# VectorE's order in the SSD steps of a two-layer diffusion backbone: the expert slots of a step ahead of its three results

## What is computed

```python
xdt = x * dt[..., None]
a = dt * a_neg;  a_cum = cumsum(a)
lmat = exp(segsum(a))                        # the decay tile of a chunk, 128 x 128 for each head
scores = einsum('bclhn,bcshn->bhcls', ch, bh) * lmat
y_diag = einsum('bhcls,bcshp->bclhp', scores, xdt)
states = einsum('bclhn,bhcl,bclhp->bchpn', bh, decay_states, xdt)
y_off  = einsum('bclhn,bchpn,bhcl->bclhp', ch, states_before, exp(a_cum))
# PEER, for each block of 128 tokens
act = gelu(einsum('thkd,td->thk', u_tab[idx], hb))
out = einsum('thk,thkd->td', gate * act, v_tab[idx])
```

## Time and profile before

| | us |
|---|---|
| median of 3 runs | 4722.75 (4718.49 to 4725.61) |
| the profiled execution | 4715.53 |
| its span on the core | 4713.7 |
| TensorE busy | 3706.6 (79%), mean granted clock 0.934 |
| VectorE busy | 3311.5 (70%) |
| ScalarE busy | 763.8 (16%) |
| GpSimd busy | 1482.1 (31%) |
| SSD steps of the sample group, layer 1 | 590.5 to 702.0 |
| SSD steps of the prompt group, layer 2 | 2407.9 to 2437.2 |
| SSD steps of the sample group, layer 2 | 2892.3 to 3003.8 |

### The profile page before, as it was taken

The page is one execution under the profiler, slowest core; times in us unless marked ns, Lnnn a source line. Parts: engine busy times, 40 slices in busy tenths (PEclk is TensorE's granted clock), DMA queues, the critical chain, the costliest instruction groups (busy, mean ns, idle before and its releaser), DMA issues.

```text
span 4713.7 us, 35962 instructions
## 1 busy us (share of the span) xinstructions
PE 3706.6 (79%) x10742; PEld 1837.6 (39%) x10742; DVE 3311.5 (70%) x8263; ACT 763.8 (16%) x2285; POOL 1482.1 (31%) x1284
## 2 busy tenths in 40 slices
PE   6578677988787778788878696788977878777776
PEld 6464434643232222235535453355422323222222
DVE  1636885677888868754574767767788787786665
ACT  0121125221010010010121112351210100101001
POOL 0001131223544435422222011213244544444432
PEclk9789798999999999999989897899999999999999
DMA  8244465777999999999979354658699999999998
GB/s 275 84 131 161 164 233 201 274 269 311 419 420 410 422 415 420 419 371 391 367 255 352 125 196 163 224 205 305 248 398 421 408 421 421 413 421 418 400 421 338
DMA packets 342147, 1497.69 MB, mean 318 GB/s; under 512 B 31424, under 2 KB 176448, under 8 KB 178112
## 3 DMA queue, kind: packets, MB, share of 16 engines
q0 software_dynamic: 184320, 1342.26, 71.0%
q1 hardware_dynamic: 157632, 153.13, 10.1%
HBM read 1491.97 MB, written 3.31 MB: 317 GB/s over the span
## 4 chain that ended last, share of the span: by engine, by line
DMA 32%; PE 31%; DVE 28%; issue 5%; ACT 4%; SPq 1%; POOL 0%; DVEq 0%; ACTq 0%; POOLq 0%
DMA uv_ring<-uv,expert_index 20%; PE expert_acc L752 13%; DMA arena<-uv,expert_index 10%; DVE uv_ring L1340 6%; PE rotating L989 3%; PE rotating L781 3%; DVE diag L1349 3%; PE rotating L815 2%; DVE arena L1340 2%; PE rotating L961 2%; DVE arena L1722 2%; DVE arena L1509 2%; DVE arena L1715 2%; DMA w_ring<-w_ada 1%; PE rotating L731 1%
## 5 line engine op out<-in xcount | busy, mean ns | idle before, releaser
L752 PE MATMUL expert_acc<-uv_ring,diag 128*128 128x512 f32 x3452 | 1736.2, 634 | 391.7 <-DVE diag L1349 382.5
L705 POOL DMA_INDIRECT uv_ring<-uv,expert_index x943 | 1091.2, 1157 | 2678.9 <-PE expert_acc L752 1942.5
L752 PEld LDWEIGHTS expert_acc<-uv_ring,diag 128*128 128x128 f32 x3452 | 632.0, 198 | 1354.1 <-DVE diag L1349 811.1
L1340 DVE CUSTOM_DVE_ANT_0 uv_ring<-uv_ring,arena 128x1024 f32<-128x1024 f32 x687 | 839.7, 1223 | 259.8 <-DMA uv_ring<-uv,expert_index 256.6
L752 PE MATMUL expert_acc<-arena,diag 128*128 128x512 f32 x1348 | 677.5, 627 | 220.2 <-DVE diag L1349 189.9
L1049 ACT ACTIVATE gelu<-u_dot 128x1 f32<-128x1 f32 x1280 | 258.8, 203 | 2789.1 <-DVE u_dot L1340 2788.5
L1349 DVE TENSOR_SCALAR diag<-const_mats,expert_gate,gelu 128x128 f32<-128x128 f32 x1200 | 436.4, 364 | 272.1 <-ACT gelu L1049 184.1
L705 POOL DMA_INDIRECT arena<-uv,expert_index x337 | 390.7, 1159 | 509.0 <-PE expert_acc L752 491.0
L752 PEld LDWEIGHTS expert_acc<-arena,diag 128*128 128x128 f32 x1348 | 238.0, 194 | 643.8 <-DVE diag L1349 422.0
L1340 DVE CUSTOM_DVE_ANT_0 arena<-arena 128x1024 f32<-128x1024 f32 x337 | 412.5, 1224 | 95.8 <-DMA arena<-uv,expert_index 94.8
L1340 DVE CUSTOM_DVE_ANT_0 uv_ring<-uv_ring,prompt_rows 128x1024 f32<-128x1024 f32 x256 | 312.4, 1220 | 104.7 <-DMA uv_ring<-uv,expert_index 104.2
(11 more groups left out here) (211 smaller groups left out, 2895.7 us busy)
## 6 DMA issues: line engine op xcount, KB each, us to landing
w_ring<-w_ada SPq DMA_DIRECT2D x66, 512.0 KB
w_ring<-w_in SPq DMA_DIRECT2D x64, 512.0 KB
w_ring<-w_pq SPq DMA_DIRECT2D x64, 512.0 KB
w_ring<-w_out SPq DMA_DIRECT2D x32, 512.0 KB
uv_ring<-w_ada SPq DMA_DIRECT2D x30, 512.0 KB, 5.8
uv_ring<-uv,expert_index POOLq DMA_INDIRECT x943
arena<-b_ada SPq DMA_DIRECT2D x48, 128.0 KB
arena<-uv,expert_index POOLq DMA_INDIRECT x337
```

The costliest lines, as they stand in the source:

```text
L705: pool.indirect_dma_start(out=UV[j], out_offset=None, in_=uv, in_offset=bass.IndirectOffsetOnAxis(ap=idxs[:, n % 2, k:k + 1], axis=0)).the ...
L752: ins = pe.matmul(acc[:, half, :], diag[:, TURN[m] % DIAGS, :], UV[SLOT_AT[m]][:, D + 512 * half:D + 512 * half + 512], start=first, stop= ...
L1340: V_.tensor_tensor_reduce(UV[j][:, 0:D], UV[j][:, 0:D], rows_of(n), 1.0, 0.0, ALU.mult, ALU.add, dots[:, m % DOTS:m % DOTS + 1]).then_inc( ...
```

## The change

One call moves: `beside.point("st", i)` on VectorE stands behind the mask of line 1580 and no longer behind the last signal of the step. So VectorE does its three dots and three diagonals of a step before it takes in yo, y and the state product. The order on TensorE, ScalarE, GpSimd and SyncE is untouched, and so is every instruction.

```diff
@@ -1578,6 +1578,7 @@
                         dve.wait_ge(*free["dd"].at(l, g, 2 * i + 1))
                         e4 = Em[i % 2].rearrange("p (g h) m -> p g h m", g=2)
                         V_.tensor_tensor(e4, e4, gm[:, b, d].unsqueeze(2).broadcast_to([P, 2, 4, P]), ALU.mult).then_inc(s_em.sem, 1)
+                        beside.point("st", i)
                         t = tile_of("yo", l, g, i)
...
@@ -1598,7 +1599,6 @@
                             chain(ins)
                         V_.tensor_copy(nw[:, 2, 2:3], nw[:, 0, 0:1]).then_inc(free["st"].sem, 1)
                         V_.tensor_copy(nw[:, 2, 3:4], nw[:, 0, 0:1]).then_inc(s_sup.sem, 1)
-                        beside.point("st", i)
```

## The result

The changed kernel takes 4736.72 us (7 runs, 4728.49 to 4740.13) against 4723.95 (7 runs) for the kernel before: ratio 1.0025, 95% interval 1.0015 to 1.0035. That is 12.8 us slower, forecast was 4.9. The sign was right and both waits that were named did appear; the size was not right. 12.8 us lies above the upper bound of the sum (11), and 4736.72 lies 0.7 us above the top of the range (4719 to 4736), which was built on a median before of 4722.75, 1.2 us less than the seven runs give. By its ratio the change is just over the 0.2% that a measurement can tell.

The account below looks back on a forecast made before the run. The SSD stage was taken as bound by a VectorE-TensorE loop, VectorE the fuller. Losses of 6.4 us (3.0 + 1.8 + 1.0 + 0.6) less 1.5 gained made 4.9 us slower: 4727.7 from a median of 4722.75, range 4719 to 4736.

Parts of the forecast that it names:

- both waits that were named: New VectorE waits in the SSD steps: on ScalarE's gelu before the second diagonal, and on gathers before the dots.
- Saved: VectorE's waits for y and the state product vanish: 0.85 us an ordinary step, 2.7 and twice 0.98 in first steps.
- The gelu wait: VectorE's second diagonal waits for ScalarE's gelu: 1.05 to 1.4 us in 12 steps, 2.2 in layer 1's first.
- The gathers: Dots wait for late rows: 1.75 us in two last steps, 2.8 last prompt step, 0.6 lost in layer 2's second.
- Rival (b): Gathers become the bound of every step: 16 us slower, 4739; chance 0.12.
- Rival (c): TensorE's clock falls after idling, decay products slow: 1.8 us on 12 steps, 22 us more, 4749; chance 0.03.
- Rival (d): ScalarE's table switch costs more than its load, 2.56 us on 12 steps: 36 us more, 4763; chance 0.02.
- (a): VectorE's waits just vanish, neither gelu nor gather late: 18 us faster, 4705; chance 0.07.
- (e): The two sides cancel, gelu comes as VectorE gets there (a wait near 0.8): 4723; chance 0.08.

Follow-up runs that it names:

- swap: Changed kernel plus one ScalarE edit: a step's gelus go ahead of the next step's exponentials; 4739.43 us, ratio 1.0029.
- two edits that it calls for: On the changed kernel: TensorE's first expert product right behind yo, and ScalarE's gelus ahead of the next exponentials; both together 4708.78 us, ratio 0.9977.
- the same TensorE edit: First expert product of a step right behind yo, ahead of the decay products; in the changed kernel 4718.11 us, ratio 0.9996.
- before_early: Kernel before the change, with only TensorE's first expert product moved right behind yo, ahead of the decay products; 4775.10 us, ratio 1.0131.

## Why the prediction was right in sign and short in size

**Saved: right.** 17.4 us predicted, 17.4 measured on lines 1587 and 1592.

**The gelu wait: right.** Predicted 1.05 to 1.4 in 12 steps, taken as 1.05. In the kernel after seven of them have 1.04 to 1.11, and three with a DMA wait in the same step 0.64 to 0.78; the third step of layer 2 has 2.80, and the second, held up by gathers, none. The first step of layer 1 has 1.79 (2.2 predicted), the first of layer 2 none, as predicted. Added in all 14.3 us, where the prediction's terms make 15.4 (12 of 1.1, and 2.2). The step came to 13.07, within the 13.0 to 13.2 named, and the load to 3.34 after line 1565 (3.35 to 3.7).

**The gathers: the step that failed.** It was priced at 6.9 us of waits (twice 1.75, 2.8 and 0.6) and measured 14.6: 4.19, 5.17 and 5.20 in the three stages. That excess of 7.7 is as large as the distance between the 4.9 of the sum and the 12.6 of the stages, in part by luck: the gelu waits came to 1.1 less than priced, and 1.1 of the 12.6 lies in none of these waits (VectorE's instructions in the stages take 1.0 us longer in all). Three things in the price were mis-sized:

- *Landing of three gathers in a row.* I took 11.4 us from the first gather's start to the third dot (5.6 for a lone one, and 2.9 for each of two more, from a stretch at 366 GB/s). The four late places show 13.5, 12.1, 13.1 and 11.1. The bytes of three came at 328 GB/s, 3.2 us each, and in two of the four some 2 us with nearly no traffic followed before the dot. A lone gather and a good stretch gave a value near the best case, not a middle one. In the ordinary step the third dot runs 12.0 after the first gather's start (638.77 to 650.79) and just doesn't wait.
- *Its start.* Taken as 5.0 after the mask's end; right in three of the four places, 6.7 in the prompt step, with TensorE's clock down.
- *Who waits.* I placed one wait at the third dot; the second dot waits too (1.04 ahead of 2.34), and in the prompt step all three do.

**Rival (b)** is half of what happened: gathers bound the last steps and the second one of layer 2's sample group, not each step (three of the 12 have waits of 0.19 to 0.38 us for them). The experiment swap shows how near it was: with ScalarE out of the way each pair of steps runs on the gathers. **Rival (c)**, the clock, was taken as all or nothing, 1.8 us on 12 steps. Ordinary steps never show it (1.85 us of idling, 1.98 for the products). It strikes behind longer waits (4.04 us idle, then 3.39 for the decay products; 3.32 idle in layer 1's last step, then 2.02 for the state product) and once, in the prompt step, where no such wait stands ahead of it. What it adds to the 12.6 us wasn't tried. **Rival (d)** fell: the second load ends at 637.14 and the gelu starts at 637.15. The Trainium skill, page ScalarE: Activation LUTs, section What ACT_TABLE_LOAD costs, adds a drain of about 1.38 us to each load; in these steps the trace shows none, with the exponentials 1.29 after their load's start and the gelu 1.29 after its. **Rivals (a) and (e)** were out with the gelu wait at 1.11.

## What to carry to other kernels

A wait that stands in a loop of several engines is exchanged, not removed, as long as the next constraint lies close behind it: here 0.85 us of waiting for y and the state product gave way to 1.11 on a gelu, and right behind that stood the gathers, so the move alone lost 13 us, with one of the two edits that it calls for it lost 14 or came out even, and with both it gained 11. Before moving work within such a step, write down for each engine when its output is wanted in the new order, and price transfers by the slowest of their kind in the trace, not by a lone one; what is wanted earlier must also be released earlier, which is TensorE's and ScalarE's order as much as VectorE's. An edit that is good in one order can be bad in another: by the stages, the same TensorE edit brings 10 us in the new order and costs 56 in the old one.

## What the hardware showed that I had not expected

- Three gathers of 1.05 MB in a row took between 11.1 and 13.5 us from the first one's start to the dot that needs the third, at 328 GB/s in the last step of layer 1's sample group and 353 in that of layer 2's while bytes flowed.
- GpSimd's instruction for a gather takes 0.94 to 0.97 us where VectorE's dot no longer runs beside it (638.77) and took 1.98 where one did; over the kernel GpSimd is busy 1451.7 us instead of 1482.1. Whether the dot is the cause wasn't tried.
- TensorE's granted clock falls within a stage after 4.04 us of idling (0.58 in the 3.4 us after 2946.30, two decay products 3.39 us, where 2.4 GHz gives 1.98) and stays up after 1.85. It fell once where TensorE had idled no more than 1.36 and 1.25 us at a time (0.50 from 2430.31 to 2433.72). In the kernel before_early, with 3.48 us of idling in the step, it is 0.80 on average over the whole step.
